# Decoder trunk step on one core: the cached sequences' value products in fp32r, with split probabilities and pages

## The reference, cut to what matters

```
ckv = concat(cache_ckv[pages].reshape(2048, 256), ckv_new)      # latent rows
kpe = concat(cache_kpe[pages].reshape(2048, 32), kpe_new)       # rotated keys
k   = rmsnorm(concat(einsum('lc,chd->lhd', ckv, w_uk), kpe))    # 8 heads, 64 + 32
s   = einsum('qhd,khd->hqk', q, k) * SCALE, masked
p   = softmax(s)
o_lat = einsum('hqk,kc->qhc', p, ckv)
o   = einsum('qhc,chd->qhd', o_lat, w_uv)
```

## Time and profile before

| what | value |
|---|---|
| runs | 1564.25, 1563.56, 1562.23 us |
| median | 1563.56 us |
| span of the profiled execution | 1561.6 us |
| its time | not listed apart; the fastest of the runs is 0.6 us above the span, the median 2.0 us |
| TensorE, VectorE, ScalarE, GpSimd busy | 1546.7, 1042.6, 631.2, 581.8 us |
| cached sequences | about 717 to 1041 us of the span |

### The profile page before, as it was taken

One profiled execution on the slowest core, in us unless ns is written; L12 is line 12 of the kernel. 1 busy time (PEld: TensorE's weight loads), 2 busy tenths in 40 slices (PEclk: granted clock), 3 DMA queues, 4 the chain that ended last, 5 costly groups with the idle time before them and its releaser, 6 DMA issues.

```text
span 1561.6 us, 31760 instructions
## 1 busy us (share of the span) xinstructions
PE 1546.7 (99%) x11182; PEld 1475.9 (95%) x11182; DVE 1042.6 (67%) x1672; ACT 631.2 (40%) x1192; POOL 581.8 (37%) x604
## 2 busy tenths in 40 slices
PE   8999999999999999999999999999999999999998
PEld 8999999999999999588988888888999999999998
DVE  4998888512269975866777777774759988885011
ACT  6444445422221242464654445552434444354110
POOL 3165555445445654320000000013551655554342
PEclk9999999999999999999999999999999999999999
DMA  6133334223223332002122222212222333342222
GB/s 173 51 101 92 94 94 124 69 80 87 80 77 103 83 112 73 1 1 72 52 62 62 61 62 62 58 45 81 82 81 58 105 94 94 94 118 67 75 82 72
DMA packets 231405, 122.29 MB, mean 78 GB/s; under 512 B 28399, under 2 KB 228311, under 8 KB 231300
## 3 DMA queue, kind: packets, MB, share of 16 engines
q1 hardware_dynamic: 230238, 120.30, 27.4%
q10 hardware_dynamic: 1070, 0.74, 0.2%
HBM read 117.79 MB, written 3.58 MB: 78 GB/s over the span
## 4 chain that ended last, share of the span: by engine, by line
PE 93%; DVE 3%; issue 1%; ACT 1%; DMA 1%; SPq 0%; DVEq 0%; ACTq 0%
PE ps L474 40%; PE ps L1439 27%; PE ps L1790 12%; PE ps L1724 4%; PE ps L1710 2%; PE ps L1581 1%; PE ps L1635 1%; PE ps L1610 1%; PE ps L1753 1%; DMA x_nat<-in_x_sample 1%; PE ps L1625 1%; PE ps L1587 1%; PE ps L1592 0%; DVE xs L1999 0%; DVE xs_raw L1984 0%
## 5 line engine op out<-in xcount | busy, mean ns | idle before, releaser
L460 POOL TENSOR_TENSOR w_lobuf<-w_rawbuf,w_hibuf 128x256 fp32r<-128x256 f32 (+2 forms) x336 | 316.8, 974 | 355.1 <-ACT w_hibuf L453 355.1
L1439 PE MATMUL ps<-xs,w 128*128 128x288 f32 x3192 | 427.5, 296 | 2.2 <-DVE w L1913 2.2
L1439 PEld LDWEIGHTS ps<-xs,w 128*128 128x128 f32 x3192 | 426.8, 188 | 2.6 <-issue 2.6
L756 POOL TENSOR_TENSOR w<-w_raw,w 128x256 fp32r<-128x256 f32 x216 | 222.6, 1062 | 222.9 <-DVE w_raw L1901 139.2
L453 ACT ACTIVATE w_hibuf<-w_rawbuf 128x1024 fp32r<-128x1024 f32 (+1 forms) x90 | 104.8, 1164 | 359.6 <-PE ps L474 358.2
L474 PE MATMUL ps<-a_hi,w_hibuf 128*128 128x288 f32 x704 | 152.6, 297 | 0.0
L474 PE MATMUL ps<-a_hi,w_lobuf 128*128 128x288 f32 x704 | 152.1, 297 | 0.0
L474 PE MATMUL ps<-a_lo,w_hibuf 128*128 128x288 f32 x704 | 150.2, 294 | 0.0
L474 PE MATMUL ps<-x_hi,w_hibuf 128*128 128x288 f32 (+1 forms) x672 | 146.1, 299 | 1.6 <-DVE w_lobuf L2073 0.8
L474 PE MATMUL ps<-x_hi,w_lobuf 128*128 128x288 f32 (+1 forms) x672 | 144.5, 296 | 0.0
L474 PE MATMUL ps<-x_lo,w_hibuf 128*128 128x288 f32 (+1 forms) x672 | 144.4, 296 | 0.0
(11 more groups left out here) (320 smaller groups left out, 2722.7 us busy)
## 6 DMA issues: line engine op xcount, KB each, us to landing
w_raw<-in_ffn_w_gu SPq DMA_DIRECT2D x76, 256.0 KB, 2.9
up_rows<-in_ffn_w_gu SPq DMA_DIRECT2D x74, 256.0 KB, 3.1
c_nat<-in_cache_ckv SPq DMA_DIRECT2D x128, 128.0 KB, 2.0
w_rawbuf<-in_w_in SPq DMA_DIRECT2D x58, 256.0 KB, 3.1
w_rawbuf<-in_ffn_w_down SPq DMA_DIRECT2D x32, 384.0 KB, 4.0
w_rawbuf<-in_ffn_w_down SPq DMA_DIRECT2D x32, 320.0 KB, 3.4
w_rawbuf<-in_ffn_w_gu SPq DMA_DIRECT2D x24, 256.0 KB, 3.3
w_rawbuf<-in_w_out SPq DMA_DIRECT2D x16, 256.0 KB, 3.1
```

The lines of the kernel that those rows point to most:

```text
L460: ins = pool.tensor_tensor(w_lobuf[:, r, part], w_rawbuf[:, r, part], w_hibuf[:, r % HIS, part].bitcast(F32), ALU.subtract)
L756: ins = pool.tensor_tensor(w7[b][:, slot, 1, part], w7_raw[b][:, slot, 1, part], w7[b][:, slot, 0, part].bitcast(F32), ALU.subtract)
L1439: mm = pe.matmul(ps[:, seven_bank(f, slot), 0:HALF], m, xs[:, slot, n, k, :], start=k == 0 and j == 0, stop=k == KH - 1 and j == 2)
```

## The change

- For the value products of `r` = 0 to 5 (done in sequences 1 to 6, `stacked(s)`), the probabilities are made twice: ScalarE's exponential writes an fp32r high part into `p_two[:, t, 0]` and the f32 value into `s_buf`; GpSimd subtracts the two into `p_two[:, t, 1]`. The 128 columns (64 high, 64 low) form one stationary tile. Its products with the pages' high parts and low parts give all four part products; rows 64 to 127 of the result are added to rows 0 to 63 after the division and the transposition.
- The pages' high parts `c_hi` are made by ScalarE, two pages at a time, in four buffers: pairs 0 to 3 at pages 2 to 5, pairs 4 to 7 at pages 11 and 12, where each waits until TensorE has used the buffer's earlier pair. The low parts overwrite the pages in place (`c_lo` has the address of `c_nat`), made by GpSimd. The new tokens have parts of their own, made once.
- TensorE's value block is cut in two: pairs 0 to 3 ahead of page 12's products, pairs 4 to 7, the new tokens and the sums ahead of page 15's; the result is transposed after page 15. `pages_used` is incremented per pair, and a group of four pages to load waits for two pairs.
- The sum of the probabilities includes the new tokens before it goes to TensorE (VectorE adds them) and is stored twice.
- GpSimd's square of the rotary keys stands behind its subtractions for `r`.
- The first two chunks of the merge weights are loaded after the values of `r` = 5; the first chunk is split in sequence 7 (ScalarE at pair 4, and the second at pair 5 where it was pair 1; GpSimd ahead of its square).
- Sequences `r` = 6 and 7 keep the old products.

```diff
+        p_two = place("p_two", [P, NP + 1, 2, HQ], F32R, ring_at)
+        c_hi = [place(f"c_hi{j}", [P, 2, KL], F32R, at) for j, at in enumerate((
+            ring_at + 4 * (NP + 1) * 2 * HQ, hi_at, hi_at + 8 * KL, tb_at + 4 * NS * NP))]
+        c_lo = place("c_lo", [P, 2, NP, KL], F32R, A0)
...
+        STACKED = NS - 2
+        PAIRS, EARLY_PAIRS = NP // 2, len(c_hi)
+        SPLITS = PAIRS + 2
+        HIGHS = PAIRS + 2
+        LATE_AT = 11
+
+        def stacked(s):
+
+            return not isinstance(s, int) or s <= STACKED
+
+        def pair_made(r, j):
+
+            return r * SPLITS + (EARLY_PAIRS + 1 if j < EARLY_PAIRS else j + 3)
+
+        def high_made(r, j):
+
+            return r * HIGHS + (j + 1 if j < EARLY_PAIRS else j + 3)
...
             load_gates(2, 4)
-            for t in range(2):
-                load_merge(t)
...
                     if used is not None:
-                        sp.wait_ge(pages_used, used + (g + 1))
+                        sp.wait_ge(pages_used, used + 2 * (g + 1))
...
-                    load_pages(i * 2 + b, b, i * 8 + 4 * (b - 2))
-
+                    load_pages(i * 2 + b, b, i * (2 * PAIRS) + (EARLY_PAIRS + PAIRS * (b - 2)))
+
+            sp.wait_ge(lat_mm, STACKED)
+            for t in range(2):
+                load_merge(t)
...
+            pool.sem_inc(pages_used, EARLY_PAIRS)
...
+            def split_pair(r, b, j):
+
+                two = slice(2 * j, 2 * j + 2)
+                pool.wait_ge(p_done, high_made(r, j))
+                pool.tensor_tensor(c_lo[:, b, two, :], c_nat[:, b, two, :], c_hi[j % EARLY_PAIRS][:, :, :].bitcast(F32), ALU.subtract)\
+                    .then_inc(split_made, 1)
+
+            def probabilities_low(r, b, half):
+
+                t = slice(half * NP // 2, (half + 1) * NP // 2)
+                pool.wait_ge(p_done, exp_made(r, half))
+                ins = pool.tensor_tensor(p_two[:, t, 1, :], s_buf[:, b, t, :], p_two[:, t, 0, :].bitcast(F32), ALU.subtract)
...
             def squares(s, b, uses, prev, nxt):
 
+                if prev and stacked(s):
+                    for j in range(EARLY_PAIRS):
+                        split_pair(s - 1, 1 - b, j)
+                    for half in range(2):
+                        probabilities_low(s - 1, 1 - b, half)
+                    for j in range(EARLY_PAIRS, PAIRS):
+                        split_pair(s - 1, 1 - b, j)
+                if not nxt:
+                    split_lo(pool, n_merge, n_merge % RAWS, KD * P)
...
+                for half in range(2):
+                    t = slice(half * NP // 2, (half + 1) * NP // 2)
+                    last = half == 1
+                    if stacked(r + 1):
+                        act.activation(p_two[:, t, 0, :], s_buf[:, b, t, :], ACT.Exp, scale=SCALE)
+                        if last:
+                            act.activation(p_two[0:TS, NP, 0, :], s_buf[0:TS, b, NP, :], ACT.Exp, scale=SCALE)
+                    ins = act.activation(s_buf[:, b, t, :], s_buf[:, b, t, :], ACT.Exp, scale=SCALE)
+                    if last:
+                        ins = act.activation(s_buf[0:TS, b, NP, :], s_buf[0:TS, b, NP, :], ACT.Exp, scale=SCALE)
+                    ins.then_inc(p_done, 1)
+                    yield
+
+            def pair_high(r, b, j):
+
+                act.wait_ge(ct_tr, r * PAIRS + (j + 1))
+                act.wait_ge(pages_used, r * PAIRS + (j + 1))
+                act.activation(c_hi[j % EARLY_PAIRS][:, :, :], c_nat[:, b, 2 * j:2 * j + 2, :], ACT.Copy).then_inc(p_done, 1)
...
+                        if prev and stacked(s):
+                            if 2 <= t < 2 + EARLY_PAIRS:
+                                pair_high(s - 1, 1 - b, t - 2)
+                            if t - LATE_AT in (0, 1):
+                                for j in range(2):
+                                    pair_high(s - 1, 1 - b, EARLY_PAIRS + 2 * (t - LATE_AT) + j)
...
+                if stacked(r + 1):
+                    for j in range(PAIRS):
+                        pe.wait_ge(split_made, pair_made(r, j))
+                        for u in range(2):
+                            t = 2 * j + u
+                            pe.matmul(ps[:, 7, 0:KL], p_two[:, t].rearrange("p h n -> p (h n)"), c_hi[j % EARLY_PAIRS][:, u, :], start=t == 0, stop=False)
+                            mm = pe.matmul(ps[:, 7, 0:KL], p_two[:, t].rearrange("p h n -> p (h n)"), c_lo[:, b, t, :], start=False, stop=False)
+                        mm.then_inc(pages_used, 1)
+                        if j < PAIRS - 1:
+                            yield
+                    for part in (new_hi, new_lo):
+                        pe.matmul(ps[:, 7, 0:KL], p_two[:, NP].rearrange("p h n -> p (h n)"), part[:, :], start=False, stop=False)
+                    pe.wait_ge(p_summed, r + 1)
+                    pe.matmul(ps[:, 7, KL:KL + 1], den_sum[:, :, :].rearrange("p h n -> p (h n)"), ones[:, 0:1], start=False, stop=True).then_inc(lat_mm, 1)
+                    yield
...
+                        if prev and stacked(s):
+                            for _ in range({12: 4, 15: 4}.get(t, 0)):
+                                next(soft)
                         cols = slice(SQ * b, SQ * b + KQ)
...
                         mm.then_inc(page_mm, 1)
+                        if prev and stacked(s) and t == NP - 1:
+                            next(soft)
```

More of the change, by code:

```diff
@@ L802, in _ @@
             pool.memset(head_ss[:, :, :, :], 1.0).then_inc(filled, 1)
-            for n in range(n_gate + KD + 2, n_merge + 1):
+            for n in range(n_gate + KD + 2, n_merge):
                 split_lo(pool, n, n % RAWS, KD * P)
@@ L841, in _ @@
             pool.wait_ge(filled, 5)
-            def squares(s, b, uses, prev, nxt):
+            for part in (p_two[TS:P, NP, :, :], new_hi[TS:P, :], new_lo[TS:P, :]):
+                pool.memset(part.bitcast(F32), 0.0).then_inc(filled, 1)
+            pool.wait_ge(filled, 8)
+            pool.tensor_copy(new_hi[0:TS, :], c_new[:, :]).then_inc(filled, 1)
+            pool.wait_ge(filled, 9)
+            pool.tensor_tensor(new_lo[0:TS, :], c_new[:, :], new_hi[0:TS, :].bitcast(F32), ALU.subtract).then_inc(filled, 1)
+            pool.wait_ge(filled, 10)
+            def split_pair(r, b, j):
[7 more added lines that the diff above has]
+                ins = pool.tensor_tensor(p_two[:, t, 1, :], s_buf[:, b, t, :], p_two[:, t, 0, :].bitcast(F32), ALU.subtract)
+                if half:
+                    ins = pool.tensor_tensor(p_two[0:TS, NP, 1, :], s_buf[0:TS, b, NP, :], p_two[0:TS, NP, 0, :].bitcast(F32), ALU.subtract)
+                ins.then_inc(split_made, 1)
+            def squares(s, b, uses, prev, nxt):
+                if prev and stacked(s):
[7 more added lines that the diff above has]
+                    split_lo(pool, n_merge, n_merge % RAWS, KD * P)
                 for g in range(NP // 4):
@@ L1570, in _ @@
             four_gates(KD + 4, q_gate3)
[L1572 to L1573 removed]
+            pe.wait_ge(small_in, 48)
             for i in range(NT):
@@ L1721, in soft_pe @@
                 yield
-                pe.wait_ge(p_done, r + 1)
+                if stacked(r + 1):
+                    for j in range(PAIRS):
[12 more added lines that the diff above has]
+                    yield
+                    pe.wait_ge(rows_in, 9 * 16)
+                    pe.wait_ge(lat_scaled, r + 1)
+                    for k in range(2):
+                        tr = pe.transpose(ps[:, 7, k * P:(k + 1) * P], o_lat[:, k * P:(k + 1) * P], ident[:, :])
+                    tr.then_inc(lat_tr, 1)
+                    yield
+                    return
+                pe.wait_ge(p_done, exp_made(r, 1))
                 for t in range(NP):
                     mm = pe.matmul(ps[0:HQ, 7, 0:KL], s_buf[:, b, t, :], c_nat[:, b, t, :], start=t == 0, stop=False)
-                    if t % 4 == 3:
+                    if t % 2:
                         mm.then_inc(pages_used, 1)
@@ L1729, in soft_pe @@
                 pe.wait_ge(p_summed, r + 1)
-                pe.matmul(ps[0:HQ, 7, KL:KL + 1], den_sum[:, :], ones[:, 0:1], start=False, stop=False)
-                pe.matmul(ps[0:HQ, 7, KL:KL + 1], s_buf[0:TS, b, NP, :], ones[0:TS, 0:1], start=False, stop=True).then_inc(lat_mm, 1)
+                pe.matmul(ps[0:HQ, 7, KL:KL + 1], den_sum[:, 0, :], ones[:, 0:1], start=False, stop=True).then_inc(lat_mm, 1)
                 yield
@@ L1763, in pe_seq @@
                         transpose_pair(s + 1, 1 - b, uses + b, 0)
-                    if prev and pp in (6, 7):
+                    if prev and not stacked(s) and pp in (6, 7):
                         next(soft)
@@ L2473, in soft_dve, with part @@
                 yield
-                dve.wait_ge(p_done, r + 1)
-                dve.tensor_reduce(den_sum[:, :], s_buf[:, b, 0:NP, :].rearrange("p t n -> p n t"), AX, ALU.add).then_inc(p_summed, 1)
+                dve.wait_ge(p_done, exp_made(r, 1))
```

(27 more changed lines are left out.)

35 lines of the change are left out of this document (20 added, 15 removed).

## The result

The changed kernel takes 1587.79 us (median of 4 runs, 1583.74 to 1588.54) beside 1563.44 us (4 runs) for the kernel before on the same chip: ratio 1.0143, 95% interval 1.0124 to 1.0162, so 22 us (by the ratio) to 24 us (by the medians) **slower**. Forecast was 1576 us, with a range of 1562 to 1586: right in its direction and in the reload, too small in its size. The median lies 1.8 us above the range, and the ratio, put on the 1563.56 us of before, gives 1585.9, at its very edge. The span of the profiled execution grew by 24.7 us, from 1561.6 to 1586.3.

A forecast was written before the change was run, and what follows sets the result against it. TensorE, busy 99% of the span, was taken as the bound; 6 x (0.43 reload net of products + 0.4 exponentials + 1.3 clock) = +12.8 us on 1561.6 gave 1574.4, plus 2.0 from span to median: 1576 us, range 1562 to 1586.

The forecast's parts named there:

- reload, less the products saved: Block-to-block interval in the cached sequences: 41.59 us instead of 41.16, +0.43 per sequence, the whole product saving eaten.
- The products: TensorE's value block, six sequences: 8.03 us removed, 4.24 added at 0.118 per product; 3.79 saved each, 22.7 in all.
- The reload: First four pages usable 9.52 us after the share's start, TensorE there after 5.27: waits 4.25 us between pages 13 and 14.
- The exponentials: ScalarE runs the exponentials twice, delaying page 9's copy and square, which TensorE's page 11 awaits: 0.4 us per sequence.
- The clock: After each of six reload waits TensorE's clock falls to half level (1.2 GHz): 1.3 us lost each, between 0 and 1.7.
- rival of a second low stretch: A second low-clock stretch follows the first because TensorE's start after the wait is broken: +23 us, 1586; chance 0.08.
- VectorE at zero: VectorE gets four small operations per sequence, 0.7 us, ahead of which it idles: taken at zero cost.
- The faster rival: Reloaded pages are there in time, TensorE doesn't wait and keeps 3.79 - 0.4 us per sequence: 1543 us; chance 0.11.

The follow-up runs named there:

- experiment 1: Changed kernel with 12 idle f32 products (24 instructions) put before the transposes of the next sequence's first pages, where TensorE waits for the reload: 1576.81 us, ratio 1.0084.
- experiment 3: Changed kernel with VectorE's probability sum moved behind the rotary scores' addition: alone 1587.47 us; also with the first page group reloaded by pairs, 1556.85 us.

## Why the prediction was right, and where its size was off

The first and the seventh block of the changed kernel:

```profile
781.02 0.38 PE L1815 MATMUL ps<-c_hi,p_two 128*128 128x256 f32 x1
...
1051.09 7.12 PE L1834 MATMUL ps<-c_nat,s_buf 128*64 128x256 f32 x32
```

The block-to-block intervals add up to 270.1 us after and 246.9 before: +23.1 of the +24.7. The seventh block, kept in its old form, and everything behind it take 0.5 less; what stands ahead of the first block is 2.05 later. By the prediction's steps:

| step | forecast, six sequences | measured, between the first and the seventh block |
|---|---|---|
| reload binds: share's start to transposes | 9.52 us | 9.65 us |
| reload, less the products saved | +2.6 | +3.4 |
| ScalarE's doubled exponentials | +2.4 | about +1.5 |
| half clock | +7.8 | +13.2 (span, experiment 1, and the trace) |
| VectorE's waits outside the reload's cover | 0 | +5.0 (page 5) |
| sum | +12.8 | +23.1 |

- **The products:** right. The instructions of L1815 and L1816 start 0.118 us apart but for the first, and the first share takes 2.0 us (1.89 forecast). The 22.7 us were taken off TensorE.
- **The reload:** right, and it is the turn. The first load is issued 2.11 us after the share's start (1.98 forecast). The forecast wait of 4.25 us is there as 3.0 for the transfer and 1.0 for VectorE ahead of it, in the mean.
- **The exponentials:** right in size, from spreading the maxima to the block 0.35 us more in the mean, 0.4 forecast; five of the six stand between the blocks of the table.
- **The clock:** that the half clock follows the waits was right, and the term was mis-sized: 2.2 us per sequence where 1.3 stood and 1.7 was the most allowed. The prediction scaled from one low stretch, of 3.4 us. Here a low stretch lasts 6.8 us in five of six sequences and 3.4 in one; it begins before TensorE is back at work in five of six and still covers 4.7 to 5.7 us of work in the five. Its rival of a second low stretch, at 0.08, comes nearest to that, but the reason it gave isn't seen: no broken start, the low clock simply goes on. That its 1586 is what came is luck in part: it had 18 us of clock for the 13.2 and nothing for VectorE's 5.0. The rows also show that a wait is not the only thing that goes with a fall: the kernel before has a second low stretch, from 718.1 to 721.5 us, which the prediction overlooked, with no wait above 0.3 us from 700 us on. The rows for it stand below the list.
- **VectorE at zero:** this step failed. "Four small operations, 0.7 us, ahead of which it idles" cost 2.4 us in two of them alone, and the taps 0.5 us more each in the mean, because GpSimd's new subtractions run beside them. GpSimd was costed by its own duration (1.04 forecast, 1.28 to 1.46 measured) and not by what it does to VectorE. Of the 11.6 us of waits from this, 6.1 were hidden by the reload (experiment 3) and 5.0 were not; 0.6 stands ahead of the first block. Its full weight, 25 us, shows only once the reload is mended.
- **The faster rival** (pages in time) was to win at a wait for the transfer below about 2 us. That didn't hold by itself: with the pages in time the kernel was still at 1572.74 us (ratio 1.0051), not at 1543, because VectorE took the place. Only with that mended too did it turn faster, and without the contention it came to 1547.65, near that rival's 1543.

The low stretches: two of the kernel before, then one of the changed kernel, at its second wait for the transfer:

```profile
18.50:21.50 3.00, 3.00 (x18) 2.98 (x16) 2.21 (x4) 2.43 (x5) 0.00 (x0) 0.50 0.53 148
718.50:721.00 2.50, 2.50 (x12) 2.17 (x12) 1.86 (x6) 1.81 (x4) 0.00 (x0) 0.50 0.11 17
```

```profile
834.50:841.00 6.50, 5.28 (x23) 5.28 (x24) 5.41 (x7) 1.31 (x3) 2.93 (x2) 0.50 0.33 91
```

What stays open: 0.6 of the 2.05 us ahead of the first block is there already at the stage's first transposes (718.12 us, 717.55 before), and another 0.6 is a wait at page 5 for VectorE, and 0.6 is the first doubled exponentials. The remaining 0.3, and why the stage starts 0.6 later, weren't separated. Nor is it known what made the low stretches of one kernel 3.4 us long and of another 6.8.

## What to carry to other kernels

When a change shortens the work between the release of a buffer and its next use, put the refill's whole path (release, issue rate of the queue, landing) beside the time that is left: here 9.6 us against 5.3 turned a saving of 22.7 us into a loss, and a wait of 3 us cost two more in clock. Work put on GpSimd was paid here by VectorE's SBUF instructions that ran beside it, so place them apart. And an edit that shows nothing alone may be worth 16 us behind another: look at which wait took its place before dropping it.

## What the runs showed of the hardware that wasn't expected

- A 64x64 addition on VectorE takes 0.22 us with GpSimd quiet and 1.20 beside its 128x512 subtractions; a tap 0.74 and 1.5. An addition or subtraction with one of its two operands in PSUM wasn't slowed (`cT_lo`, 682 and 685 ns).
- Idle products in the wait (24 instructions, 2.6 us) kept the clock at 1.00 and gave 11 us, though they compute nothing.
- The length of a wait alone didn't tell whether the clock fell. In the changed kernel it fell at waits of 2.5 to 3.4 us, but not at one of 2.37 (947.89 us). With the reload by pairs it fell three times (near 839, 938 and 1010 us), behind waits of 1.9, 2.4 and 2.4, and not at three others of 1.8 to 1.9.
- Nor did it tell for how long. With the sum moved alone, six waits of 3.8 to 4.3 us had low stretches of 6.8 us in five sequences and 3.4 in one; with the short subtractions on the changed kernel, six waits of 3.9 to 4.5 us had 3.4 in five and 6.8 in one.
